# Feature splits, token differences and up banks moved to other places at both ends of six feed-forward stages

## The reference

```python
def swiglu(x, w_gate, w_up, w_down):
    return (jax.nn.silu(x @ w_gate) * (x @ w_up)) @ w_down
# first block, per layer:   x = _layernorm(ALPHA * x + swiglu(x, ...), ...)
# second block, per layer:  h = x + 0.5 * swiglu(rms_norm(x, ffn1_norm[l]), ...)
...
#                           x = h + 0.5 * swiglu(rms_norm(h, ffn2_norm[l]), ...)
```

## Time and profile before

| | |
|---|---|
| time, median of 3 runs | 3161.9 us (3161.71 to 3161.94) |
| time of the profiled execution | 3159.76 us |
| its span | 3158.0 us |
| TensorE, matmuls | busy 3094.3 us, 98% of the span, 17462 instructions |
| VectorE | busy 1796.2 us, 57% |
| ScalarE | busy 923.0 us, 29% |
| GpSimd | busy 1926.9 us, 61% |
| DMA | mean 90 GB/s |
| mean granted TensorE clock | 0.991 |

### The profile page before, as it was taken

How to read it: one execution, slowest core, us unless ns; L and a number is a source line. 1 busy time by engine, 2 the same in 40 slices (tenths; PEclk the granted TensorE clock), 3 DMA queues, 4 the chain that set the end, 5 groups by cost and what they waited for, 6 DMA issues and landing times.

```text
span 3158.0 us, 46571 instructions
## 1 busy us (share of the span) xinstructions
PE 3094.3 (98%) x17462; PEld 2656.2 (84%) x17462; DVE 1796.2 (57%) x2750; ACT 923.0 (29%) x1800; POOL 1926.9 (61%) x2485
## 2 busy tenths in 40 slices
PE   8999999999999999899999999999999999999999
PEld 7878998898789988799788789988899787789977
DVE  5577455175774442777517567761577436567741
ACT  4454222054542220522212332220322112332210
POOL 5347547673474476455878375577555877385484
PEclk9999999999999999999999999999999999999999
DMA  5112322231123322132232123222222232123222
GB/s 185 46 41 74 113 100 94 94 108 41 48 71 110 106 94 91 63 111 101 90 112 89 54 81 107 100 94 100 94 100 93 99 111 85 42 96 106 100 94 67
DMA packets 83063, 284.53 MB, mean 90 GB/s; under 512 B 9532, under 2 KB 15069, under 8 KB 82653
## 3 DMA queue, kind: packets, MB, share of 16 engines
q1 hardware_dynamic: 77484, 273.70, 25.5%
q10 hardware_dynamic: 5424, 8.79, 0.8%
HBM read 278.79 MB, written 3.67 MB: 89 GB/s over the span
## 4 chain that ended last, share of the span: by engine, by line
PE 91%; DVE 5%; ACT 2%; POOL 1%; issue 1%; DMA 0%; DVEq 0%; ACTq 0%; POOLq 0%
PE bank_v L588 20%; PE bank_v L589 19%; PE bank_v L590 19%; PE bank_s L864 6%; PE bank_s L866 6%; PE bank_s L865 6%; DVE h_lo L2190 2%; PE bank_a L588 2%; PE bank_a L589 2%; PE bank_a L590 2%; PE bank_v L987 1%; PE bank_a L966 1%; PE bank_s L1127 1%; POOL w_lo L562 1%; PE bank_s L1005 1%
## 5 line engine op out<-in xcount | busy, mean ns | idle before, releaser
L562 POOL TENSOR_TENSOR w_lo<-raw,w_hi 128x512 fp32r<-128x512 f32 x808 | 1131.9, 1401 | 64.6
L558 POOL TENSOR_TENSOR zero<-zero 128x1 f32<-128x1 f32 x808 | 284.3, 352 | 622.0 <-PE bank_v L590 466.9
L588 PE MATMUL bank_v<-xn_hi,w_hi 128*128 128x512 f32 (+1 forms) x1680 | 642.1, 382 | 9.8 <-DVE xn_lo L1900 8.4
L589 PE MATMUL bank_v<-xn_lo,w_hi 128*128 128x512 f32 (+1 forms) x1680 | 635.6, 378 | 0.0
L590 PE MATMUL bank_v<-xn_hi,w_lo 128*128 128x512 f32 (+1 forms) x1680 | 635.2, 378 | 0.0
L559 POOL CAST w_hi<-raw 128x512 fp32r<-128x512 f32 x808 | 556.5, 689 | 0.1
L588 PE MATMUL bank_v<-h_hi,w_hi 128*128 128x512 f32 (+1 forms) x1122 | 427.7, 381 | 20.3 <-DVE work L1966 15.9
L589 PE MATMUL bank_v<-h_lo,w_hi 128*128 128x512 f32 (+1 forms) x1122 | 426.0, 380 | 0.0
L590 PE MATMUL bank_v<-h_hi,w_lo 128*128 128x512 f32 (+1 forms) x1122 | 425.7, 379 | 0.0
L588 PEld LDWEIGHTS bank_v<-xn_hi,w_hi 128*128 128x128 f32 x1680 | 317.2, 189 | 69.4 <-issue 8.9
L590 PEld LDWEIGHTS bank_v<-xn_hi,w_lo 128*128 128x128 f32 x1680 | 317.0, 189 | 59.8
(11 more groups left out here) (414 smaller groups left out, 6363.0 us busy)
## 6 DMA issues: line engine op xcount, KB each, us to landing
raw<-in_w_stream SPq DMA_DIRECT2D x516, 512.0 KB, 3.3
rope<-in_rope ACTq DMA_DIRECT2D x2, 1024.0 KB, 5.8
da_v<-t_rows ACTq DMA_DIRECT2D x2, 1024.0 KB, 7.4
out<-resid SPq DMA_DIRECT2D x8, 256.0 KB, 2.3
t_rows<-t_row ACTq DMA_DIRECT2D x1, 1536.0 KB, 6.7
resid<-in_x ACTq DMA_DIRECT2D x5, 256.0 KB, 7.5
mla_v<-in_alibi ACTq DMA_DIRECT2D x2, 512.0 KB, 7.7
resid<-in_x SPq DMA_DIRECT2D x3, 256.0 KB, 9.5
```

Source lines behind the costliest of these rows:

```text
L558: pool.tensor_tensor(zero[:, 1:2], zero[:, 0:1], zero[:, 0:1], ALU.add)
L562: ins = pool.tensor_tensor(w_lo[:, u, cut], raw[:, u, cut], w_hi[:, u, cut].bitcast(F32), ALU.subtract)
L588: pe.matmul(out, lhs_hi, rhs_hi, start=first, stop=False)
L589: pe.matmul(out, lhs_hi, rhs_lo, start=False, stop=False)
```

## The change

Four things move; no operation of the engines is added or taken away. TensorE's queue gets five more waits per pair.

**The end.** In the last pair ACT begins to round features as soon as the product that used their place is done: 2, 3, 4, 5 after p7, 0 and 1 after p5, 6 and 7 after p4, the rest after p3. DVE subtracts six of them between the steps that combine the products (`H_AHEAD`), in the order of `H_ORDER`, and then takes the first up bank after eight and the second after twelve subtractions (`H_UPS`).

**The start in the first block.** Differences 0, 2 and 1 are formed and rounded ahead of the first products and Silus, difference 3 after them; the four subtractions for `t_lo` go behind `first(1, 0)` and between the parts of the first pair.

**The start of the first stage of the second block (`kept`).** `scaled_x` is formed by ACT ahead of the root of the norm. DVE forms the four differences and `t_lo` 0 and 2 while it waits for the spread factors (in `factor`), and makes the parts of the first pair, with `t_lo` 1 and 3 between them, before `first(1, 0)`.

**Order of the parts.** A22 goes from second to fourth place, and `RAW_FREE` with it from 2 to 4: POOL's wait at line 551 now ends after S23, S1 and A22. TensorE waits for the token parts at the product that needs them rather than once ahead of the loop.

```diff
-LO_PARTS = ("a", "A22", "S23", "S1", "S4")
+LO_PARTS = ("a", "S23", "S1", "A22", "S4")
+H_ORDER = (2, 3, 4, 5, 0, 1, *range(6, FC))
+H_AHEAD = dict(u3=2, c22=1, c11=1, c21=0, c12=2)
+H_UPS = (8, 12)
 RAW_FREE = LO_PARTS.index("A22") + 1
...
                 split("S23")
+                pe.wait_ge(*x_lo.after((tag, "t", 1)))
                 multiply(bank_22, s2, t2).then_inc(*multiplied.done((tag, at, "p6")))
+                pe.wait_ge(*x_lo.after((tag, "t", 2)))
                 multiply(bank_21, s3, t3).then_inc(*multiplied.done((tag, at, "p7")))
                 split("S1")
+                pe.wait_ge(*x_lo.after((tag, "t", 0)))
...
                 pe.wait_ge(*combined.after((tag, at, "u3")))
+                pe.wait_ge(*x_lo.after((tag, "t", 3)))
+                split("A22")
...
+            def hidden_hi_early(tag, ready, ends, fs):
+
+                act.wait_ge(*multiplied.after((tag, "last", ends)))
                 act.wait_ge(*ready("pair", 1))
-                for f in range(FC):
...
+                for f in fs:
+                    hidden_hi(tag, f)
...
+                tokens_hi(tag, 0, 2, 1)
                 gate(0, 0)
                 gate(0, 1)
-                tokens_hi(tag)
+                tokens_hi(tag, 3)
                 gate(1, 0)
                 first_pair_hi(tag)
...
+                if kept:
+                    for c in range(DC):
+                        keep_scaled_x(C2["ffn1"], c)
                 root(stats, 1)
...
-            def factor(tag):
+            def factor(tag, ahead=lambda: None):
 
                 dve.wait_ge(*sums.after((tag, "sum")))
                 inverse_root(tag, 1, D, 1e-6)
+                ahead()
                 dve.wait_ge(*sums.after((tag, "spread", 0)))
...
+            def hidden_lo(tag):
+
+                done = []
+
+                def some(n):
+                    for f in H_ORDER[len(done):len(done) + n]:
+                        dve.wait_ge(*x_hi.after((tag, "h", f)))
+                        dve.tensor_tensor(h_lo[:, f, :], hidden[:, f, :], h_hi[:, f, :].bitcast(F32), ALU.subtract
+                                          ).then_inc(*x_lo.done((tag, "h", f)))
+                        done.append(f)
...
+                def rest(finish):
+                    for k, at in enumerate(H_UPS):
+                        some(at - len(done))
+                        finish(k)
+                    some(FC - len(done))
...
+                token_sum(tag, resid, 0, 2, 1)
                 first(0, 0)
                 first(0, 1)
-                token_sums(tag, resid)
+                token_sum(tag, resid, 3)
                 first(1, 0)
-                first_pair(tag)
+                token_lo(tag, 1, 2)
+                first_pair(tag, lambda name: token_lo(tag, dict(S1=0, A22=3)[name]) if name in ("S1", "A22") else None)
                 first(1, 1)
...
+                def kept_tokens():
+                    tokens()
+                    token_lo(tag, 0, 2)
 
-                first(1, 0)
-                first_pair(tag)
+                if kept:
+                    first_pair(tag, lambda name: token_lo(tag, 1, 3) if name == "S23" else None)
+                    first(1, 0)
```

More of the change, by code:

```diff
@@ L1531, in ffn @@
                 pair("last", None)
[L1532 removed]
+                hidden_hi_rest(tag, ready)
             def keep_scaled_x(column, c):
@@ L1556, in pair @@
                     keep_p1(tag, at)
-                    if at != "last":
+                    if at == "last":
+                        for ends, fs in (("p7", H_ORDER[0:4]), ("p5", H_ORDER[4:6]), ("p4", H_ORDER[6:8])):
+                            hidden_hi_early(tag, ready, ends, fs)
+                    else:
                         act.wait_ge(*multiplied.after((tag, at, "p2")))
@@ L1579, in ffn_scaled @@
                 pair("last", None)
-                hidden_hi(tag, lambda at, k: product.after((tag, at, k)))
+                hidden_hi_rest(tag, ready)
             def write_sink(key, n, k):
@@ L2142, in pair_lo, with first_pair @@
                                   ).then_inc(*weights_summed.done((tag, at, "S4")))
[L2143 to L2157, removed]
+            def pair_lo(tag, at, *names):
+                _, b = pair_slots(tag)
+                for name in names:
+                    lo, whole, hi = dict(S23=(s_lo[:, 0:2, :], s_sum[:, 0:2, :], s_hi[:, 0:2, :]),
+                                         S1=(w_lo[:, b, 0:KEPT], w_sum[:, b, 0:KEPT], w_hi[:, b, 0:KEPT]),
+                                         A22=(w_lo[:, b, KEPT:UNIT], raw[:, b, KEPT:UNIT], w_hi[:, b, KEPT:UNIT]),
+                                         S4=(s_lo[:, 2, :], s_sum[:, 2, :], s_hi[:, 2, :]))[name]
+                    dve.wait_ge(*weights_hi.after((tag, at, name)))
+                    if name == "S23":
+                        dve.wait_ge(*weights_summed.after((tag, at, "S4")))
+                    dve.tensor_tensor(lo, whole, hi.bitcast(F32), ALU.subtract).then_inc(*weights_lo.done((tag, at, name)))
+            def first_pair(tag, between=lambda name: None):
                 dve.wait_ge(*w_used.after((tag, "up1", 0)))
@@ L2160, in first_pair, with combine_early @@
                 pair_a_lo(tag, "first")
-                pair_lo(tag, "first")
+                pair_last_sum(tag, "first")
+                for name in LO_PARTS[1:]:
+                    pair_lo(tag, "first", name)
+                    between(name)
             p1, u2, u3 = (parts[:, n, :] for n in range(3))
-            def combine_early(tag, at):
+            def combine_early(tag, at, ahead=lambda name: None):
                 dve.wait_ge(*act_step.after((tag, at, "p1")))
@@ L2182, in combine_12, with ahead @@
                 dve.tensor_tensor(work[:, 0, HALVES[1]], u2, bank_12, ALU.add).then_inc(*c12_read.done((tag, at, "c12")))
-            def last_hidden(tag, finish):
-                for f in range(FC):
-                    if f in (FC // 2 - 1, FC - 2):
-                        finish(f // (FC // 2))
-                    dve.wait_ge(*x_hi.after((tag, "h", f)))
-                    dve.tensor_tensor(h_lo[:, f, :], hidden[:, f, :], h_hi[:, f, :].bitcast(F32), ALU.subtract
-                                      ).then_inc(*x_lo.done((tag, "h", f)))
+            def hidden_lo(tag):
[6 more added lines that the diff above has]
+                        done.append(f)
+                def ahead(name):
+                    some(H_AHEAD.get(name, 0))
+                def rest(finish):
[3 more added lines that the diff above has]
+                    some(FC - len(done))
+                return ahead, rest
             def ffn(tag):
@@ L2226, in ffn, with tokens @@
                 pair("last", None)
-                last_hidden(tag, lambda k: finish("last", k, slice(FC - 2 + k, FC - 1 + k)))
+                rest(lambda k: finish("last", k, slice(FC - 2 + k, FC - 1 + k)))
             def ffn_scaled(tag, stats, kept=False):
-                factor(stats)
+                def tokens():
+                    dve.wait_ge(*act_step.after(("scaled_x", C2[tag], DC - 1)))
+                    token_sum(tag, scaled_x, 0, 2, 1, 3)
+                def kept_tokens():
+                    tokens()
+                    token_lo(tag, 0, 2)
+                factor(stats, kept_tokens if kept else lambda: None)
                 def times_up(k, at, gate, up, done):
```

91 lines of the change are left out of this document (59 added, 32 removed).

## The result

The kernel after takes 3107.74 us (median of 4 runs, 3107.27 to 3108.57), the kernel before in the same session 3161.81 us (3161.32 to 3161.94). The ratio is 0.983, 95% interval 0.9813 to 0.9847. The change gains 54.1 us, 1.7%; the prediction said 52.4 us and 3109.5 us. The profiled execution went from 3159.8 to 3107.3 us, by 52.5 us.

A forecast was written before the change was run, and what follows sets the result against it. TensorE, busy in 98% of the span, bounds the kernel; only gaps and slow stretches, 56.2 us, can be won. 29.3 + 12.3 + 10.9 = 52.5 us off 3159.8 gives 3107.3, plus 2.1 for the median: 3109.5 us, range 3104 to 3124.

The forecast's parts named there:

- five waits at the ends: Feed-forward stage ends: of TensorE's waits, five were said to belong there, line 588 with `h_hi` before the first down chunk.
- Down starts: Six first down chunks: waits on `finish` vanish; 20.2 us of waits, six times 0.15, 9.4 clock, less 1.2: 29.3 us.
- the tail of `h_lo`: First down chunk: last subtractions level with TensorE's need; 0.3 us of waiting allowed in each of four stages, 1.2 us.
- First-block starts: Two stage starts of the first block: POOL's halves no longer slowed by DVE, its waits vanish; 12.3 us gained.
- The new Silu waits: First-block starts: ACT rounds three differences ahead of the first Silu, so TensorE waits 0.55 and 1.2 us.
- Kept start: Second block's first stage: first pair's part a ready 3 us before TensorE wants it; 9.8 + 0.15 + 1.8 - 0.9 = 10.9 us.
- `keep_p1`: Second block's first stage: this ACT copy stands behind two Silus waiting for DVE, making p2 wait 0.9 us.
- Loop: 48 laps: POOL's later release and five added waits per gate stage on satisfied counts cost 0.
- Rival (d): TensorE's queue: 270 added waits lie open, slower; at 0.3 us each 3190 us; chance 0.03.
- Clock: Behind nearly each of TensorE's gaps at stage starts and ends the granted clock falls; 15.6 us lost in sum.
- Rival (a): Places of the new small waits: each brings the lower clock again, 6.3 us not gained, 3116 us; chance 0.12.

The follow-up runs named there:

- ends alone: Kernel before with only the edits of the six stage ends (early splits, H_ORDER, up banks after 8 and 12 subtractions): 3127.88 us, ratio 0.990.
- alone: Kernel before with the kept start's edits, the new order of the parts and TensorE's added waits: 3151.84 us, ratio 0.9975.
- the order alone: Kernel before with only the new order of the parts and TensorE's added waits, ends and starts as before: 3157.84 us, ratio 0.9994.
- the run with 540 more instructions: Kernel after with each TensorE wait for a part of the gate weights stated five times over: 3108.71 us.

## Why the prediction was right

The waits, their places and the clock behind them were read rightly from the rows. That the total of 52.5 us came out to the tenth is luck: the down starts gave 2.1 us more than forecast and the kept start 2.0 us less. (The prediction's opening speaks of five waits at the ends; its rows and its sum have six.)

**Down starts.** Predicted 29.3, traces 31.4, ends alone 32.5 us. Waits 21.1 as forecast. The bank was read 4.5 us ahead of TensorE, the estimate was 3.9 in the second block. The rest of the difference is the matmuls behind each gap (0.15 us six times) and the tail of `h_lo`. That was called level with 1.2 us lost and is level with nothing lost; the run without early splits shows that it is the nearest bound. With 0.3 us of room, one early split fewer, at 1.1 us, would lie open by this sum; no run tried one.

**First-block starts.** Predicted 12.3, traces 12.3. The mechanism (DVE's long operations hold up POOL) is shown by the run with `t_lo` moved back alone. The equality of the sums has luck in it. Without the stretches far from the starts the two gain 12.5 us: at the first start 5.0 of POOL's three waits, 1.7 of clock and 0.3 unexplained, less 1.1 for the Silu; at the second 4.6 of its two waits, 2.9 of clock and 0.2 unexplained, less 1.1. A stray stretch at 278 in before adds 1.5 us, one at 828 in after takes 1.7 off. The new Silu waits were forecast as 0.55 and 1.2 and are 0.96 each.

**Kept start.** Predicted 10.9, traces 8.9, alone 6.0 us (8.5 less the 2.5 of the order alone). The preparation went as worked out: six operations of 1.6 us each (1.54 estimated), part a ready at 1297.1, gates at 1300.0, 2.9 us ahead (3 estimated). The term that was mis-sized is `keep_p1`, "until about 1325.6, and p2 wants it at 1324.7: 0.9 us". It measured 1.94 us, and `u3` behind it 0.6 us. Even that is the mild case: by the runs above it is 2.95 us and a fall of the clock whenever no stray stretch delays TensorE ahead of it. ScalarE in that place:

```profile
1303.77 0.64 ACT L1581 ACTIVATE work<-work 128x512 f32<-128x512 f32 x1 [4.89 <-DVE work L2001]
1304.31 0.58 ACT L1564 ACTIVATE work<-bank_a 128x512 f32<-128x512 f32 x1
1306.90 0.63 ACT L1581 ACTIVATE work<-work 128x512 f32<-128x512 f32 x1 [2.01 <-DVE work L2001]
1307.43 0.36 ACT L1487 ACTIVATE parts<-bank_s 128x256 f32<-128x256 f32 x1
```

The copy had its product from 1301.4 on and stood behind two Silus that waited for VectorE. VectorE's two products for `first(1, 0)` and `first(1, 1)` took 1.75 and 1.61 us instead of 0.69, because POOL, let go at 1302.67, works beside them; I had costed them as if POOL were quiet. Moving the copy forward alone would not help: VectorE gets to `u2` and `u3` only at 1309.2, while p4 wants `u3` at about 1307. This was read from the timelines; no run tried it.

**Loop.** Predicted 0, 0. Rival (d) fell by the run with 540 more instructions at no cost in the loop. At the price that the Trainium skill gives (Advanced Engine Details and Errata, Network/Comms) they would have made an estimated 27 to 54 us; the measured median rose by 0.9 us, five gate stages by nothing and the kept one by 0.4 us.

**Clock.** Rival (a), that the short new waits keep the lower level, is answered by the table of gaps: 0.96 us never brings it, 1.94 to 2.1 us at `keep_p1` didn't in seven traces, 3.0 us did in three of three. In after the wait stayed short of that, by the luck of the stretch at 1278.

## What to carry to other kernels

When a bank's release and a row of splits share one engine's queue, count the whole queue up to the last split against the consumer's last use, not only up to the release: moving the release without the splits won about 3 of 31 us here, since the rest came back as waits inside the chunk, while six splits moved into gaps won it all, wherever the release stood. An engine's idle stretch is the place for work that slows a neighbour; the same four subtractions cost 4 us in one place and nothing ten microseconds later. A term for the clock belongs to gaps of TensorE of about 2 us and more and to shorter ones close together, and gains ahead of a start that another engine bounds are lost in its wait.

## What the runs showed of the hardware

The granted clock falls in portions of 1.7 us, also where TensorE counts as busy throughout (at 36, 828 and 1278 in after, 0.72 over 6 us). These stray portions stand at few places: of 29 in the 14 traces, 7 at 36 to 38, 4 at 277 to 278, 5 at 828 to 831, 4 at 893 to 903 with a double one at 895, and 8 at 1278 to 1299. Ahead of each, and over less than 2 us before it, TensorE ran matmuls that count as busy but are small: 24 of 33 rows ahead of 36, 22 to 24 of a single column ahead of 278 and 893 to 903, 8 of a single column behind a wait ahead of 828 and 1278. The same matmuls stand in the traces without a fall there, and no run changed them, so that they are the cause is not shown. One to three portions are the size of the spread of the kernel before, 3157.7 to 3162.3 us; that they make it was not shown either, since only one execution of each kernel has a trace. Waits on satisfied counts in TensorE's queue cost nothing measurable while matmuls run ahead of them, 90 instructions per stage in under 0.01 us; behind a wait that had kept TensorE idle, four more lay open with 0.22 us. And a POOL instruction on a 128x1 tile grows from 0.19 to 1.17 us beside VectorE's 128x1024 operations.
